# First block's shift and scale: the conditioning vector as the stationary operand, two tiles ahead

## The reference, cut to what matters

```
mod = silu(c) @ ada_w[0] + ada_b[0]          # 9 vectors of 1024: sh1, sc1, g1, ...
y = rmsnorm(h, ffn1_pre_g) * (1 + sc1) + sh1 # rmsnorm: h * rsqrt(mean(h*h) + eps) * g
y = (silu(y @ w_gate) * (y @ w_up)) @ w_down # ffn1; h = h + 0.5 * g1 * rmsnorm(y)
```

## Time and profile before

| | |
|---|---|
| three runs | 2378.53 us median (2377.41 to 2379.94) |
| the profiled execution | 2381.1 us, its span 2379.3 us |
| PE / VectorE / ScalarE busy | 98% / 56% / 35% |
| mean granted TensorE clock | 0.985 |
| first unit's first matmul starts | 27.2 us |
| first `linear` matmul starts | 60.26 us |

### The profile page before, as it was taken

How to read it: one execution, slowest core, us unless ns; L and a number is a source line. 1 busy time by engine, 2 the same in 40 slices (tenths; PEclk the granted TensorE clock), 3 DMA queues, 4 the chain that set the end, 5 groups by cost and what they waited for, 6 DMA issues and landing times.

```text
span 2379.3 us, 27595 instructions
## 1 busy us (share of the span) xinstructions
PE 2323.7 (98%) x11154; PEld 1922.7 (81%) x11154; DVE 1336.2 (56%) x1987; ACT 835.5 (35%) x1265; POOL 210.3 (9%) x177
## 2 busy tenths in 40 slices
PE   8999999999999999999999999999999989999998
PEld 6888888877788888888788888888877767888887
DVE  7654548486238455547643576664466664644343
ACT  3322223423334322223543343322344443433221
POOL 0000004021014000003110100000121111000001
PEclk7999999999999999999999999999999999999999
DMA  8766632311212356541332246664131111433331
GB/s 315 245 201 205 197 122 80 106 37 45 62 54 71 98 187 219 192 135 53 107 98 63 63 142 213 210 215 131 45 115 58 54 44 55 147 128 97 96 100 36
DMA packets 81951, 288.07 MB, mean 121 GB/s; under 512 B 9105, under 2 KB 11281, under 8 KB 81825
## 3 DMA queue, kind: packets, MB, share of 16 engines
q1 hardware_dynamic: 81104, 284.74, 37.4%
q10 hardware_dynamic: 720, 1.57, 0.2%
HBM read 284.18 MB, written 2.10 MB: 120 GB/s over the span
## 4 chain that ended last, share of the span: by engine, by line
PE 88%; DVE 7%; ACT 3%; issue 1%; POOL 0%; DMA 0%; SPq 0%; DVEq 0%; ACTq 0%; POOLq 0%
PE bank L280 23%; PE bank L282 23%; PE bank L281 23%; PE bank L471 2%; DVE wlo L1519 1%; PE bank L424 1%; PE bank L425 1%; PE bank L403 1%; PE bank L404 1%; PE bank L405 1%; PE bank L506 1%; PE bank L429 1%; ACT whi L949 1%; DVE attd L1887 1%; PE bank L316 1%
## 5 line engine op out<-in xcount | busy, mean ns | idle before, releaser
L1519 DVE TENSOR_TENSOR wlo<-raw,whi 128x1024 fp32r<-128x1024 f32 (+1 forms) x370 | 474.6, 1284 | 355.4 <-ACT whi L949 355.1
L280 PE MATMUL bank<-yhi,whi 128*128 128x512 f32 (+1 forms) x1686 | 661.4, 392 | 4.5 <-DVE wlo L1519 3.7
L282 PE MATMUL bank<-yhi,wlo 128*128 128x512 f32 (+1 forms) x1686 | 651.8, 387 | 0.0
L281 PE MATMUL bank<-ylo,whi 128*128 128x512 f32 (+1 forms) x1686 | 651.4, 386 | 0.0
L949 ACT ACTIVATE whi<-raw 128x1024 fp32r<-128x1024 f32 (+1 forms) x370 | 385.2, 1042 | 315.2 <-PE bank L282 247.3
L280 PEld LDWEIGHTS bank<-yhi,whi 128*128 128x128 f32 x1686 | 317.4, 188 | 86.2 <-issue 21.1
L282 PEld LDWEIGHTS bank<-yhi,wlo 128*128 128x128 f32 x1686 | 317.5, 188 | 64.9
L281 PEld LDWEIGHTS bank<-ylo,whi 128*128 128x128 f32 x1686 | 317.7, 188 | 61.6 <-issue 0.7
L280 PE MATMUL bank<-mlp_ahi,whi 128*128 128x512 f32 (+1 forms) x552 | 206.6, 374 | 0.0
L281 PE MATMUL bank<-mlp_alo,whi 128*128 128x512 f32 (+1 forms) x552 | 206.2, 374 | 0.0
L282 PE MATMUL bank<-mlp_ahi,wlo 128*128 128x512 f32 (+1 forms) x552 | 206.2, 374 | 0.0
(11 more groups left out here) (333 smaller groups left out, 2860.6 us busy)
## 6 DMA issues: line engine op xcount, KB each, us to landing
raw<-in_ada SPq DMA_DIRECT2D x152, 512.0 KB, 4.5
raw<-in_ffn_up SPq DMA_DIRECT2D x88, 512.0 KB, 4.4
raw<-in_mlp_up SPq DMA_DIRECT2D x64, 512.0 KB, 3.6
raw<-in_mlp_dn SPq DMA_DIRECT2D x64, 512.0 KB, 3.6
raw<-in_ffn_dn SPq DMA_DIRECT2D x32, 512.0 KB, 3.7
raw<-in_w_dqkv SPq DMA_DIRECT2D x24, 512.0 KB, 3.6
first<-in_ada SPq DMA_DIRECT2D x16, 512.0 KB, 15.1
raw<-in_ffn_dn SPq DMA_DIRECT2D x16, 384.0 KB, 3.5
```

What stands on the lines that cost most here:

```text
L280: e.matmul(out, wh, xh, start=first, stop=False)
L281: e.matmul(out, wh, xl, start=False, stop=False)
L282: mm = e.matmul(out, wl, xh, start=False, stop=last)
L1519: e.tensor_tensor(k.wlo[:, what % NW, 0:width], raw[:, 0:width], k.f(k.whi[:, what % NW, 0:width]), ALU.subtract).then_inc(*sig.up("wlo", ...
```

## The change

1. `ROWS` replaces `SHIFTS`: PE now computes shift tiles 1 to 7 and scale tiles 1 to 3 (`ROWS[0]`, `ROWS[1]`); VectorE's `ada` keeps scale tiles 0 and 4 to 7 and shift tile 0.
2. Their form is turned round. `first_rows` takes one column of silu(c), repeated 32 times, as the stationary operand and the weights as the moving one; slice kt goes to partitions 32*(kt % 4) on, so that four partial sums lie in four groups of 32 partitions. ScalarE copies them out of PSUM (`first_row`), and `first_columns` turns the row into a column and adds the four parts with a matmul against a constant column of 1/32. Rows of tile n + 2 are issued before tile n, their columns between the two groups of tile n.
3. PE sums the squares itself, tile by tile (`totals`): from the fourth square on as they come, 8 calls of `column` in place of one; VectorE's seven additions go. Warming is 4 calls in place of 8.
4. `crow` is loaded third on SP, ahead of the odd x tiles, and its silu runs before the squares; the load of the root's table follows the squares.
5. The raw tiles of units 0 to 3 are loaded behind the pairs of modulation tiles 0 to 3, and `whi`/`wlo` of units 0 to 3 come one a tile (`prep_to`). On ScalarE `whi(u)` for u = 1 to 3 then stands behind `first_row(u + 1)`; before, unit 1's stood behind `yhi(0)` alone.

```diff
-SHIFTS = range(1, 5)
+ROWS = (range(1, 8), range(1, 4))
@@ Pe.four
             if before:
                 before(n)
             for kt, group in ((n, us[0:2]), (n - lag, us[2:4])) if lag else ((n, us),):
+                if between and group[0] > us[0]:
+                    between(n)
@@ Pe
+    def first_rows(self, n):
+        out = k.banks.at("rows")
+        w.wait_ge(k.s_first[n], 32)
+        w.wait_ge(*sig.on("sil"))
+        if n > 2:
+            w.wait_ge(*sig.on("row", n - 2))
+        for v in range(2):
+            if n not in ROWS[v]:
+                continue
+            c = slice(256 * (n % 2) + 128 * v, 256 * (n % 2) + 128 * v + 128)
+            for kt in range(8):
+                q = slice(32 * (kt % 4), 32 * (kt % 4) + 32)
+                mm = self.e.matmul(out[q, c], k.sil[:, kt:kt + 1].to_broadcast([128, 32]),
+                                   k.first_ada[v][n][:, 128 * kt:128 * kt + 128], start=kt < 4, stop=kt >= 4)
+        mm.then_inc(*sig.up("rows", n))
+    def first_columns(self, n):
+        out = k.banks.at("vec", n % 2)
+        w.wait_ge(*sig.on("row", n))
+        for v in range(2):
+            if n in ROWS[v]:
+                mm = self.e.matmul(out[:, 8 * v + n:8 * v + n + 1], k.first_row[:, n % 2, v, :],
+                                   k.cst[:, PART_C:PART_C + 1], start=True, stop=True)
         mm.then_inc(*sig.up("vec", n))
@@ Pe.totals
-        self.w.wait_ge(*self.sig.on("dsum", st, 7))
-        self.column(out, 0, self.k.tm(0), True, True).then_inc(*self.sig.up("tot", st))
+        for n in range(NT):
+            self.w.wait_ge(*self.sig.on("sq", st, n if n > 3 else 3))
+            mm = self.column(out, 0, self.k.tm(n), n == 0, n == NT - 1)
+        mm.then_inc(*self.sig.up("tot", st))
@@ Pe.program
-        self.warm(8)
+        self.warm(4)
         self.totals("start")
         self.root("start", 0)
-        for n in SHIFTS[0:2]:
-            self.shift(n)
+        self.first_rows(1)
+        self.first_columns(1)
@@ Act.first_norm
-            self.prep_to((0, 1, 1, 2, 3, 3, 3, 3)[n])
+            self.prep_to((0, 1, 2, 3, 3, 3, 3, 3)[n])
+            if n == 0:
+                self.first_row(1)
 ...
+            if n < NT - 2:
+                self.first_row(n + 2)
+    def first_row(self, n):
+        k, half, wd = self.k, 256 * (n % 2), 256 if n in ROWS[1] else 128
+        self.w.wait_ge(*self.sig.on("rows", n))
+        if n > 2:
+            self.w.wait_ge(*self.sig.on("vec", n - 2))
+        self.e.activation(k.first_row[:, n % 2, :, :].rearrange("p v f -> p (v f)")[:, 0:wd],
+                          k.banks.at("rows")[:, half:half + wd], k.ACT.Copy)
@@ Act.program
+        w.wait_ge(k.s_c, 16)
+        e.activation(k.crow[:, :], k.crow[:, :], k.ACT.Silu).then_inc(*sig.up("crow", 0))
         for n in range(NT):
             w.wait_ge(k.s_tile[n], 16)
-            if n == 7:
-...
             self.square("sq", ("start", n), k.tm(n)[:, 0:S], k.h[:, n, :])
+        self.ready_root()
@@ Dve.first_norm
-            self.add("start", n, k.tm(n)[:, 0:S])
         self.ada(1, 0)
         self.ada(0, 0)
-        self.ada(1, 1)
         self.root("start")
+        self.prep_to(0)
@@ Dve.first_norm, for each n
             if n == 0:
-                self.prep_to(0)
-            if n + 2 not in SHIFTS and n + 2 < NT:
-                self.ada(0, n + 2)
+                self.prep_to(1)
+            if n + 2 < NT and n + 2 not in ROWS[1]:
+                self.ada(1, n + 2)
             low(n)
-            if n + 2 < NT:
-                self.ada(1, n + 2)
-            if n < 4:
-                self.prep_to((1, 1, 2, 3)[n])
+            if 0 < n < 3:
+                self.prep_to(n + 1)
@@ Sp.program
+        e.dma_start(k.crow[:, :], k.dram["c"]).then_inc(k.s_c, 16)
         for n in range(1, NT, 2):
             e.dma_start(k.h[:, n, :], k.dram["x"][:, n, :]).then_inc(k.s_tile[n], 16)
-        e.dma_start(k.crow[:, :], k.dram["c"]).then_inc(k.s_c, 16)
-            for u in ((), (0, 1), (), (2,), (3,), (), (), ())[n]:
+            for u in ((0,), (1,), (2,), (3,), (), (), (), ())[n]:
```

More of the change, by code:

```diff
@@ L36 @@
 ]
[L38 removed]
+IDENT, ONES, PERM, CAUS, CNEG, INVF_C, EPS_C, HPI_C, SEL_C, PART_C, NCONST = 0, 128, 256, 384, 512, 640, 641, 642, 643, 647, 648
 MIX_ORDER = [("mif", 0, 1), ("hq", 0, 4), ("hf", 0, 4), ("hi", 0, 4)]
@@ L70, in constants @@
     c[:, HPI_C] = math.pi / 2
+    c[:, PART_C] = 1 / 32
     for h in range(4):
@@ L408, in tokens, with four @@
             mm.then_inc(*sig.up("lin", u))
-    def four(self, tags, x, hi, lag=0, before=None):
+    def four(self, tags, x, hi, lag=0, before=None, between=None):
         w, sig, e, k = self.w, self.sig, self.e, self.k
@@ L443, in four @@
                         low(at, u)
-    def shift(self, n):
+    def first_rows(self, n):
         w, sig, k = self.w, self.sig, self.k
-        out = k.banks.at("shift", n % 3) if n > 3 else self.bank("shift", n % 3, hold=True)
-        if n > 3:
-            w.wait_ge(*sig.on("mod0", n - 3))
+        out = k.banks.at("rows")
         w.wait_ge(k.s_first[n], 32)
         w.wait_ge(*sig.on("sil"))
-        for kt in range(8):
-            mm = self.e.matmul(out[:, n:n + 1], k.first_ada[0][n][:, 128 * kt:128 * kt + 128], k.sil[:, kt:kt + 1],
-                               start=kt == 0, stop=kt == 7)
+        if n > 2:
[10 more added lines that the diff above has]
+    def first_columns(self, n):
+        w, sig, k = self.w, self.sig, self.k
+        out = k.banks.at("vec", n % 2)
[4 more added lines that the diff above has]
+                                   k.cst[:, PART_C:PART_C + 1], start=True, stop=True)
         mm.then_inc(*sig.up("vec", n))
@@ L526, in up @@
                 done = 4 if gated else 3
-                if not gated:
-                    self.first_units([tag] * 3, y, "yhi", {"mlp0": "gla", "mlp1": "diff"}[st])
[L529 to L534, removed]
+                if st == "ffn1":
+                    self.four([tag] * 4, y, "yhi", 3, self.rows_ahead, self.columns_ahead)
+                    k.banks.let_go(("rows",))
+                    for i in range(2):
+                        k.banks.let_go(("vec", i))
+                elif gated:
+                    self.four([tag] * 4, y, "yhi")
+                else:
+                    self.first_units([tag] * 3, y, "yhi", {"mlp0": "gla", "mlp1": "diff"}[st])
             for _ in range(done, n):
@@ L552, in ffn, with rows_ahead, columns_ahead @@
             self.bridge(st)
-    def shift_ahead(self, n):
-        if n + 2 in SHIFTS[2:]:
-            self.shift(n + 2)
+    def rows_ahead(self, n):
+        if n < NT - 2:
+            self.first_rows(n + 2)
+    def columns_ahead(self, n):
+        if n < NT - 2:
+            self.first_columns(n + 2)
     def decay(self, st, q, kk, bg):
@@ L915, in program @@
         self.w.wait_ge(k.s_cst, 16)
-        self.warm(8)
+        self.warm(4)
         self.totals("start")
         self.root("start", 0)
-        for n in SHIFTS[0:2]:
-            self.shift(n)
+        self.bank("rows", hold=True)
+        for i in range(2):
+            self.bank("vec", i, hold=True)
+        self.first_rows(1)
+        self.first_columns(1)
         self.ffn("ffn1", FFN_GROUPS, True)
@@ L1094, in first_norm @@
                               bias=k.mod[:, n:n + 1]).then_inc(*sig.up("yhi", "ffn1", n))
+            if n < NT - 2:
+                self.first_row(n + 2)
[5 more added lines that the diff above has]
+        self.e.activation(k.first_row[:, n % 2, :, :].rearrange("p v f -> p (v f)")[:, 0:wd],
+                          k.banks.at("rows")[:, half:half + wd], k.ACT.Copy).then_inc(
+            *self.sig.up("row", n, bank=("rows",) if n == 7 else None))
     def ffn(self, st, counts, gated):
@@ L1688, in first_norm @@
         for n in range(NT):
+            vec = k.banks.at("vec", n % 2)
             w.wait_ge(*sig.on("bias1"))
[L1690 to L1697, removed]
+            if n:
+                w.wait_ge(*sig.on("vec", n))
+            else:
+                w.wait_ge(*sig.on("ada", 0, 0))
+            if n not in ROWS[1]:
+                w.wait_ge(*sig.on("ada", 1, n))
+            e.scalar_tensor_tensor(A[:, n:n + 1], vec[:, 8 + n:9 + n] if n in ROWS[1] else k.mod[:, 8 + n:9 + n],
+                                   one[:, n:n + 1], g[:, n:n + 1], ALU.add, ALU.mult).then_inc(*sig.up("coef", "ffn1", n))
+            e.tensor_tensor(k.mod[:, n:n + 1], vec[:, n:n + 1] if n else k.mod[:, 0:1], k.pc("ada_b", n),
+                            ALU.add).then_inc(*sig.up("mod0", n, bank=("vec", n % 2) if n > 5 else None))
             w.wait_ge(*sig.on("spread", "R", "start"))
@@ L2442, in build_program @@
             k.first_ada = [[first[:, v, n, :] for n in range(NT)] for v in range(2)]
+            k.first_row = sb("first_row", [128, 2, 2, 128], fp32, s)
         hidden("ffn1", FFN_GROUPS)
@@ L2581, in lay_out @@
     w = x["ada_w"][0]
```

(2 more changed lines are left out.)

12 lines of the change are left out of this document (3 added, 9 removed).

## The result

| | us | runs |
|---|---|---|
| before | 2378.24 median (2375.76 to 2381.18) | 19 |
| after | 2384.51 median (2380.81 to 2390.65) | 19 |
| ratio | 1.0024, 95% interval 1.0018 to 1.0030 | |

The forecast of 2381.0 is 3.5 us too low, and the range 2374.5 to 2393 holds the time. The profiled execution after took 2387.47 us (span 2385.7, before 2379.3).

A forecast was written before the change was run, and what follows sets the result against it. PE was taken as the bound from the first plain unit on; first unit at 28.9, 33.0 us behind it and 1.0 at half clock end at 62.9 against 60.43, 2.5 later: 2381.0, range 2374.5 to 2393.

The forecast's parts named there:

- case A: Course as worked out, chance 0.45: packed rows, later root, new stalls; 2378 to 2384, full clock back before 35 us.
- the sum: From first unit at 28.9: matmuls 21.8, rows 2.5, columns 1.7, stalls 7.0, plus 1.0 at half clock; `four` ends 62.9.
- The way to the root: PE's 64 column instructions, from 12.1 to 22.4 us with a clock fall, put the spread's end at 24.6, 3.9 later.
- the rest ends near 11: PE's remaining four warming calls were to end near 11 us, before the sums of squares start at 12.1.
- The rows: `first_rows` on PE ahead of the units: tile 1's 32 instructions 1.7 us at half clock; 2.3 us of the loss regained.
- the quarter of the full price: Row instructions on four partition groups run at the same time, each costing a quarter of 0.211 us at half clock.
- The wait at the second unit: PE stands 2.4 us for `wlo(1)`, behind the row copy and `whi(1)`; then waits of 0.6, 1.9 and 2.1 us.
- I add 1.0 for a part still at half: Allowance of 1.0 us behind the first unit for PE work at half clock, which should end earlier than before.
- 62.9: Predicted end of `four` in us, against 60.43 before: 2.5 us later.
- B: Rival, chance 0.22: rows run one after another at full price, about 12 us over the likeliest case, 2393.
- C: Rival, chance 0.15: rows packed, but the clock returns no sooner than before, at 43.4; end near 65, 2383.5.
- D: Rival, chance 0.12: clock holds through the 64 columns, first unit at 23.2, end 3.5 us earlier, 2375.0.

The follow-up runs named there:

- the second execution: Profiled execution of the changed kernel measured again with no edit, beside the others on one chip: 2385.55 us, ratio to before 1.0026.
- rows alone: Changed kernel with parts 3 and 5 undone (parts 1, 2 and 4 stay), measured twice: 2376.40 and 2375.05 us, ratios to before 0.9988 and 0.9985.
- dense matmuls between the columns: Changed kernel with one warming call (two 512-column matmuls on constants) behind each of the first seven tiles' columns: 2384.81 us, ratio to before 1.0020.
- `whi` earlier: Changed kernel with ScalarE making `whi` of units 1 to 3 one tile earlier, ahead of the row copy: 2380.32 us, ratio to before 0.9999.
- both edits: Changed kernel with VectorE adding the squares again (8 warming calls) and `whi` of units 1 to 3 one tile earlier: 2378.08 us, ratio to before 0.9990.

## Why the prediction was off in size

The mechanism of case A was right, and so was its direction: later than before through the sums on PE, with part of it given back by the packed rows, and a new wait at the second unit. Its own range (2378 to 2384) ended 0.5 us short of the median; the whole range held it. Several terms of the sum were mis-sized, and some of them cancelled.

- **The way to the root.** `crow` landed at 8.4 (8.9 predicted), the fourth square ended near 11.5 (12.1). The estimate "the rest ends near 11" failed in the profiled execution: the warming ran to 12.9. Its instructions there follow one another after 0.85 us, only the last after 0.43, so nearly all of it ran at half clock. (That is read from the distances alone: the granted clock of these windows is given as 1.00.) The sums started at 12.87 in place of 12.1, in the second execution at 11.53, and their length, 10.3 us predicted, was 11.0 and 9.0. The spread came at 24.42 and at 21.11, around the 22.9. The whole of part 3, 3.9 us predicted, measured 4.0 us added to the kernel before and 4.8 taken from the one after. The trace of the first of these agrees less well: added alone, part 3 moved the spread by 1.84 us and the plain unit by 2.75.
- **The rows.** 32 at half clock took 1.86 us from start to next start (29.81 to 31.67), 1.7 predicted; the quarter of the full price holds, whether by the groups side by side or by the narrower load. 16 take 0.57 at full clock (29.74 to 30.31 in rows alone): the difference of 0.44 for 16 instructions leaves 0.13 us a batch for the changeover and all else that doesn't grow with the rows, an estimate. The Trainium skill's TensorE: Matmul & The Clock Gate, Part 3: Packing small matmuls, gives 2.38x for three column groups; no run here has three, and the four here gave 3.5x. The Trainium skill's TensorEngine Tiling (Array Packing), Key Properties, says a change of mode drains the engine; no run here shows the drain by itself, and by the estimate it costs at most the 0.13.
- **The wait at the second unit.** Released by `wlo`, as said; predicted 2.4, shown as 1.56 with nothing else of PE's between 32.9 and 34.45. The prediction took 0.45 us of it as covered by unit 0's two matmuls; at half clock they cover 1.2, and with a full clock (dense matmuls between the columns) the wait is 2.04. The later ones, predicted 0.6, 1.9 and 2.1, were 0.16, 0.31 and 1.68. At full clock throughout (dense matmuls between the columns) the stretch from first unit to plain unit takes 64.03 - 30.11 = 33.9, where 33.0 stood in the sum; with `whi` earlier, also at full clock, 60.51 - 30.32 = 30.2. So the order on ScalarE costs 3.7 us without any fall of the clock.
- **The stretch behind the first unit.** The sum had a first unit at 28.9 and then 26.0 us of matmuls, 7.0 of waits and "I add 1.0 for a part still at half": 34.0. The profiled execution had the first unit at 31.67 (2.8 more) and again 34.0 behind it, but that agreement is luck. Its waits come to 3.7. At full clock the matmuls alone take 28.0 (`whi` earlier, 30.2 less 2.2 of waits) to 28.4 (dense matmuls between the columns, 33.9 less 5.6), 2.0 to 2.4 more than the sum had. That leaves 1.9 to 2.3 for the lower clock in place of 1.0. The second execution had the first unit at 28.36 (0.5 less), but 37.1 behind it with 4.1 of waits, so 4.6 to 5.0 for the lower clock. This is the term that was most too small; both ends are 2.6 to 2.8 us over 62.9.
- **The clock's second fall.** The clock did come back by 35 in the first execution (case A's sign), and only at 37.1 in the second, and in both it fell again for 3.4 us, which no case had. In the profiled execution that was at 36.3, behind a stretch in which PE had stood and waited for `whi`, `wlo` and `yhi` (2.44 us busy of the 4 from 32 to 36). Waiting alone doesn't bring it: with dense matmuls between the columns PE waits 5.6 us at these units, and the clock stays at 1.00. What does bring it is open.
- **The rivals.** B was excluded by the quarter price. C needed the clock down without a break to 43; it came back at 32.9 and 37.1. D fell with the clock at 15.8: the Trainium skill's TensorE: Matmul & The Clock Gate, section The HAM clock gate, read as any busy PE, isn't borne out here either, for PE was busy 4.00 of 4 us around the fall.

Added up by ratios, starting from the kernel before: rows alone -2.9 or -3.6. Part 5 on top of them (which gives the changed kernel with part 3 undone, +1.0) costs 3.8 to 4.5. Part 3 on top of that costs 4.8, and the sum is the change's 5.7 (it has to be, since each step starts where the last ends). Roughly in these places the prediction had -2.3, +0.9 and +3.9. The largest gap, though hardly clear of the noise, is at part 5. The sum had the new waits almost paid for by an earlier end of the half clock, and the clock didn't give that much back. At full clock the order on ScalarE alone costs 3.7 us from first unit to plain unit (33.9 with it, 30.2 with `whi` earlier); moving `whi` was worth 6.0 in the changed kernel and 3.3 with part 3 undone. Which share of the 6.0 is the second fall isn't settled: the experiment that removed the wait removed the fall too.

The best version measured is rows alone, 2375 to 2376, 0.12 to 0.15% faster than before and 9 us faster than after. That is below what the prediction called a difference, though its two intervals leave out no change.

## What to carry to other kernels

Work moved onto the engine that bounds the kernel has to be paid there in full; that the engine it was taken from was busy is no gain as long as nobody waited for it, as with VectorE's additions here. A copy that feeds the next step but one shouldn't stand ahead of the split that the next matmul waits for. A change with several parts is best measured part by part: here the rows gained about 3 us, the sums on PE lost 4 to 5, the new order of loads and splits about 4, and the early `crow` did nothing, each give or take 2 to 3 us.

## What the runs showed of the hardware

- A row of one-column fp32 matmuls on 128 x 128 weights keeps PE and its weight loads busy 4.00 of 4 us and the granted clock falls to the lower of its two levels all the same, 2.9 and 5.1 us after its start in two executions of one kernel; with two 512-column matmuls behind every eight it stayed at 1.00.
- Rows in fp32 onto four groups of 32 output partitions, with a stationary operand of 32 columns, take 1.01 us for 32 instructions, against 3.58 onto all 128 with one of 128 columns, both at full clock.
- The time of one kernel varies by 5.4 us before and by 9.8 us after (lowest to highest of 19), and a gain ahead of the units isn't carried whole to the end of every execution. With both edits the plain unit stands 4.0 us earlier, the end 1.7. In between the matmuls' lead changes in steps, where one execution's clock falls and the other's doesn't. Windows of 25 us, the kernel before and then both edits:

```profile
1920.00:1945.00 25.00, 20.83 (x108) 14.78 (x105) 19.11 (x46) 13.29 (x30) 5.50 (x4) 1.00 0.14 43
```

```profile
1920.00:1945.00 25.00, 23.09 (x105) 16.66 (x104) 17.39 (x44) 12.23 (x29) 3.81 (x3) 0.80 0.07 22
```

There the edited kernel's clock is at 0.80 in a place that no edit touched. That such falls make up the spread of the times is inferred from these single executions and wasn't tested by itself.
